# Hybrid mixer of a one-core, three-layer kernel: convolution taps from PSUM, and side work queued at other steps

## The chip, the cores and the metric

The kernel runs on one core of a Trainium2 chip as a single program. The metric is device time in microseconds (us) of that core. Before the change the median of three runs is 1608.9 us (1607.36 to 1610.53). Engines are named as the profile names them: PE is TensorE (PEld its weight loads), DVE is VectorE, ACT is ScalarE, POOL is GpSimd, SP is SyncE, which issues most DMAs.

## The reference, cut to what matters

Three layers follow each other on 256 tokens of width 1024, float32: a hybrid mixer (with 16 meta tokens ahead, so 272 positions), a PEER layer that gathers 256 rows of a 128 MB table per token, and a two-layer block of retention and stick-breaking attention. The change lies in the mixer alone:

```python
proj = hn @ w_in
q, k, v, g_out, g_low, z, xbc, dt_raw, gate_a, gate_b = split_cols(proj, IN_SPLITS)
o = gla_chunked(...)                                  # gated linear attention, 4 heads
o = rmsnorm(o, gla_norm_w) * jax.nn.silu(hd(g_out, GLA_DV))
y_a = o.reshape(Bsz, L, GLA_VW) @ w_up_gla
xbc = jax.nn.silu(causal_dwconv(xbc, conv_w, conv_b)) # 4 taps per channel
xs, Bm, Cm = split_cols(xbc, (SSD_D_INNER, SSD_BC, SSD_BC))
y = ssd_chunked(xs * dt, a, Bm, Cm) + d_skip * xs     # state space model, 4 groups of 8 heads
y = rmsnorm(y * jax.nn.silu(z))                       # per group
y_b = y @ w_up_ssd
mixed = jax.nn.sigmoid(gate_a) * y_a + jax.nn.sigmoid(gate_b) * y_b
h = h + mixed @ w_out
```

`causal_dwconv` forms, for each of 3072 channels, the sum over four taps of the input shifted by 3, 2, 1 and 0 positions times a weight, plus a bias.

## The kernel before, in words

The kernel streams its weights through the core as chunks of 128x1024 float32. SP loads a chunk, ACT copies it to a rounded half (`whi`, L221), DVE forms the remainder (`wlo`, L222), and PE multiplies each of its eight 128x128 blocks three times (`triple`, L260: high by high, high by low, low by high). The split of a chunk is issued four chunks ahead of its use. A chunk of kind T (`stream_T`) puts 24 matmuls of 272 or 256 columns into a PSUM bank, one of a ring of four (banks 0 to 3); a chunk of kind N (`stream_N`) makes 12 matmuls of 512 columns into two banks. When a bank is complete, a function (`use`) issues the work that empties it and returns the point from which the bank is free again.

The rest of the mixer (everything that isn't a product with streamed weights) is written as Python generators, the **sides**. Each `yield` ends a step; `side_step` runs the next step of the first side in the list, after a chunk, and, if `ring["steps"]` is 2, also in its middle. All engines take their instructions in the order in which this program issues them, so the number of `yield`s between two pieces of side work says how many half chunks of streamed work PE has between them. `until(key)` runs steps at once until that piece of work has been issued.

The order of the chunks in the mixer: 17 T chunks (small projections, k, q, v), 8 N chunks (g_out), 8 T chunks for B and C of the state space model, 32 T chunks in which the 16 gates and the 16 channel tiles of `xs` alternate (`GATES_XS`: 6 gates, then 10 times xs and gate, then 6 xs), 8 T chunks (`w_up_gla`), 16 N chunks (z), 16 T chunks (`w_up_ssd`, the second up-projection) and 8 N chunks (`w_out`).

The sides that the change touches, in their order:

- `gla_side`: the chunked linear attention. L588 to L598 form scaled q and k on DVE (`prod` is the last, L598); `attention(i)` multiplies them on PE (40 rows of 128x64, L319), ACT and DVE mask the scores (L633 to L636), PE multiplies them by v; then norms (L654, `rstd`, L660) and `features`, which turns the result on PE (`tr`, L322) and splits it into XH and XL.
- `conv` (a `use`): for a finished bank of B, C or xs, ACT copies the bank to the buffer XP behind three zeros (L716), ACT writes the last tap and the bias (L718), and three DVE instructions add the taps that look back, read from XP (L720). The bank is free after L718. A silu (L710) follows at the next chunk's `use`.
- `first_side` and `decays(g)`: 16 Abs (L757), one Exp (L762) and two products (L765) that build the decay masks M of a group.
- `ssd_side(g)`, for g = 0 to 3, queued when the fourth xs tile of group g is done: three `turn`s of x on PE (L322), the DVE products with dt (L797, L800, L802), L815 for the state, the state and output matmuls, and L826 to L843 on DVE. It also steps `decays(g + 1)`.
- `use_z`: silu of z (L895), product (L899), squares (L900), then `y_side(g)`: `rstd`, two diagonal matrices (L334, L335), and `turned`, eight matmuls whose results are split into the inputs of `w_up_ssd`.

## Time and profile before

| what | value |
|---|---|
| median of the runs shown | 1608.9 us |
| the profiled execution's own time | 1608.27 us |
| its span, first to last instruction | 1606.5 us |
| PE busy / DVE busy / ACT busy, share of the span | 86% / 67% / 46% |
| mean granted TensorE clock | 0.958 of full |

The span has three parts. The mixer and the projections run from 0 to about 487 us; from there to about 1130 us the PEER layer gathers table rows (DMA engines full, some 420 GB/s); the second block follows. In the rows, `idle before <-releaser` in square brackets is the time that an engine stood still before an instruction and the instruction that ended this wait.

### The profile page before, as it was taken

Reading aid. Unit: us, or ns where it says so; the run is one execution under the profiler, and the core shown is the slowest. Engines: PE = TensorE matmul, PEld = TensorE weight load, DVE = VectorE, ACT = ScalarE, POOL = GpSimd, SP = SyncE. Lnnn points to the kernel's source line nnn. Section 1 sums busy time; section 2 is a strip of 40 time slices with the busy share of each in tenths; the row PEclk is TensorE's granted clock in tenths of the full one; section 3 lists DMA queues with packets and bytes.
Section 4 is the critical chain, followed back from the end, with each engine's and each line's share of the span. In section 5 each row is a group of like instructions: output and inputs, shape, how many; then the busy total and the mean of one; then the engine's idle time right before and its main releaser. Section 6 shows DMA issues by size and latency. Waiting matters only on the chain. (4 is left out here: it accounts for less than half of the span.)

```text
span 1606.5 us, 18967 instructions
## 1 busy us (share of the span) xinstructions
PE 1379.1 (86%) x6549; PEld 993.4 (62%) x6549; DVE 1080.7 (67%) x2061; ACT 736.5 (46%) x1276; POOL 301.8 (19%) x260
## 2 busy tenths in 40 slices
PE   6998979999998787777777877778899999899987
PEld 5987978888988433233333333323497787888766
DVE  5767467875678787677777777665695465645554
ACT  5665777747454322222222222212454475567853
POOL 0000000000003564444444444443100000000000
PEclk9998999999999899989999999999999999899989
DMA  6452444444558999999999999999664456354442
GB/s 225 122 183 84 153 132 142 138 141 156 182 200 326 411 421 421 422 422 420 422 421 421 422 421 422 422 420 422 251 202 155 133 184 206 124 155 146 144 128 79
DMA packets 77806, 417.70 MB, mean 260 GB/s; under 512 B 8768, under 2 KB 8832, under 8 KB 44688
## 3 DMA queue, kind: packets, MB, share of 16 engines
q0 software_dynamic: 36864, 268.45, 40.3%
q1 hardware_dynamic: 40848, 148.06, 28.9%
q8 instruction: 52, 0.85, 0.2%
q14 instruction: 42, 0.34, 0.1%
HBM read 415.39 MB, written 1.08 MB: 259 GB/s over the span
## 5 line engine op out<-in xcount | busy, mean ns | idle before, releaser
L319 PE MATMUL ps<-AR 128*128 128x512 f32 (+6 forms) x1160 | 363.6, 465 | 106.5 <-ACT AR L1211 71.8
L222 DVE TENSOR_TENSOR wlo<-raw,whi 128x1024 fp32r<-128x1024 f32 x257 | 311.7, 1222 | 170.5 <-ACT whi L221 167.9
L319 PEld LDWEIGHTS ps<-AR 128*128 128x128 f32 (+2 forms) x1160 | 191.1, 198 | 269.5 <-issue 127.1
L221 ACT ACTIVATE whi<-raw 128x1024 fp32r<-128x1024 f32 x257 | 269.4, 1054 | 119.4 <-PE ps L260 99.3
L260 PE MATMUL ps<-XH,whi 128*128 128x256 f32 (+1 forms) x1032 | 306.6, 297 | 4.7 <-DVE XL L330 2.4
L319 PE MATMUL ps<-SLAB,AR 128*128 128x512 f32 x516 | 247.3, 633 | 66.7 <-ACT AR L1211 66.6
L260 PE MATMUL ps<-XL,whi 128*128 128x256 f32 (+1 forms) x1032 | 297.2, 288 | 0.0
L260 PE MATMUL ps<-XH,wlo 128*128 128x256 f32 (+1 forms) x1032 | 297.1, 288 | 0.0
L1176 POOL DMA_INDIRECT AR<-in_peer_uv,C x127 | 148.2, 1167 | 658.0 <-DVE C L1130 486.3
L319 PEld LDWEIGHTS ps<-SLAB,AR 128*128 128x128 f32 x516 | 101.2, 200 | 209.3 <-issue 120.3
L260 PEld LDWEIGHTS ps<-XH,whi 128*128 128x128 f32 x1032 | 201.1, 195 | 12.8 <-DVE XL L330 5.1
L260 PEld LDWEIGHTS ps<-XL,whi 128*128 128x128 f32 x1032 | 200.7, 194 | 0.9 <-issue 0.7
L1185 DVE CUSTOM_DVE_ANT_0 SLAB<-SLAB,AR 128x1024 f32<-128x1024 f32 x129 | 156.7, 1222 | 65.9 <-DMA SLAB<-in_peer_uv,C 65.9
L260 PEld LDWEIGHTS ps<-XH,wlo 128*128 128x128 f32 x1032 | 200.3, 194 | 0.0
L260 PE MATMUL ps<-whi,XH 128*128 128x512 f32 x480 | 197.4, 411 | 0.0
L1185 DVE CUSTOM_DVE_ANT_0 AR<-AR 128x1024 f32<-128x1024 f32 x127 | 154.3, 1222 | 55.4 <-DMA AR<-in_peer_uv,C 55.4
L260 PE MATMUL ps<-wlo,XH 128*128 128x512 f32 x480 | 188.7, 393 | 0.0
L260 PE MATMUL ps<-whi,XL 128*128 128x512 f32 x480 | 188.5, 393 | 0.0
L1176 POOL DMA_INDIRECT SLAB<-in_peer_uv,C x129 | 153.4, 1189 | 173.6 <-PE ps L319 131.8
L1211 ACT ACTIVATE AR<-C 128x128 f32<-128x128 f32 x254 | 84.0, 392 | 170.7 <-DVE C L1199 149.1
L1194 ACT ACTIVATE C<-C,SM 128x4 f32<-128x4 f32 (+2 forms) x72 | 21.4, 297 | 295.3 <-DVE C L1185 295.2
L260 PEld LDWEIGHTS ps<-whi,XL 128*128 128x128 f32 x480 | 90.8, 189 | 20.3
(243 smaller groups left out, 1187.8 us busy)
## 6 DMA issues: line engine op xcount, KB each, us to landing
raw<-in_stream SPq DMA_DIRECT2D x257, 512.0 KB, 4.2
AR<-scr SPq DMA_DIRECT2D x8, 512.0 KB, 5.2
SLAB<-in_peer_uv,C POOLq DMA_INDIRECT x129, 28.4
AR<-in_rows SPq DMA_DIRECT2D x4, 512.0 KB
AR<-in_peer_uv,C POOLq DMA_INDIRECT x127, 28.0
AR<-in_con SPq DMA_DIRECT2D x1, 1280.0 KB, 7.2
AR<-in_xin SPq DMA_DIRECT2D x2, 512.0 KB, 5.2
AR<-in_xin SPq DMA_DIRECT2D x1, 1024.0 KB, 8.7
```

Source lines behind the costliest of these rows:

```text
L221: a = A(lambda e: e.activation(h[:, :], r, ACT.Copy), loaded[i], free, chain=False)
L222: b = V(lambda e: e.tensor_tensor(l[:, :], r, h[:, :].bitcast(F32), ALU.subtract), a, loaded[i], free, chain=False)
L260: tok = PE(lambda e, s=s, m=m, n=n: e.matmul(out_ap, s, m, start=first and n == 0, stop=last and n == 2), *(after if n == 0 else ()), sign ...
L319: return PE(lambda e: e.matmul(out_ap, l, r, start=start, stop=stop, skip_group_check=onto), *after, signal=sig)
L1176: G(lambda e: e.indirect_dma_start(slots[j], None, peer_uv, bass.IndirectOffsetOnAxis(ap=col, axis=0)).then_inc(s, 16), idx_pt[m // 16], f ...
L1185: dot_pt[m] = V(lambda e: e.tensor_tensor_reduce(u, u, HN[:, i, :], 1.0, 0.0, ALU.mult, ALU.add, AV[:, i, at:at + 1]), uv_in[m], chain=False)
L1194: gelu_pt[ms[0]] = A(lambda e: e.activation(CC[:, i, c], AV[:, i, c], ACT.Gelu_apprx_tanh, scale=SM[:, 24 + i:25 + i]), dot_pt[ms[-1]])
L1211: a = A(lambda e: e.activation(d, ident, ACT.Copy, scale=CC[:, i, c]), c_ready, dg_free.get(m - 4), chain=False)
```

## The change

The change has four parts.

1. `conv` no longer copies the bank. The XP buffer, its zeros and L716 go; the three taps read the PSUM bank `o` itself, with outputs shifted by 3, 2 and 1 positions, and the bank is free after the last of them.
2. `stream_T` can run a third step in a chunk, after its sixth block, where `ring["steps"]` is 3. It is set to 3 when the first group of the state space model is queued, and back to 2 ahead of the second up-projection. In N chunks there are still two steps.
3. `yield`s are added: two after `prod`, one ahead of each `features` in `gla_side`, three at the start of each `ssd_side` and six inside it, two in `y_side` for the first three groups.
4. `until("yT7")` is called at the end of z, so the second `y_side` is issued there at the latest, and ahead of the last group's norm.

```diff
--- before.py
+++ after.py
@@ -287,6 +287,8 @@
                                 while mid:
                                     mid.pop(0)()
                                 side_step(2)
+                            if k == 5:
+                                side_step(3)
                         used[i] = tok
                         if kg == kt - 1:
                             bank_free[b] = use(o, tok)
@@ -598,8 +600,8 @@
             prod = V(lambda e: e.tensor_tensor(chunked(qS[:, :, :], 1), qE1[:, :, :, :],
                                                chunked(GX[:, :, X], 0)[:, :, :, 63:64].broadcast_to([128, 4, 2, 64]), ALU.mult))
             att_zero = V(lambda e: e.memset(attS[64:128, :, :, 0:64], 0.0))
-            yield
-            yield
+            for _ in range(4):
+                yield
 
             def features(i, v):
                 for g in range(2):
@@ -640,6 +642,7 @@
                 yield
                 if i == 1:
                     yield
+                    yield
                     yield from held
                 for h in range(4):
                     o = ps[5 + h // 2][:, (h % 2) * 256:(h % 2) * 256 + 256]
@@ -664,6 +667,7 @@
                     held = features(i, v)
             yield
             yield
+            yield
             yield from features(1, v)
 
 
@@ -683,7 +687,6 @@
 
         BT = place("BT", 22224, 4 * T).rearrange("p (g t) -> p g t", g=4)
         CT = place("CT", 23312, 4 * T).rearrange("p (g t) -> p g t", g=4)
-        XP = place("XP", 24400, 552).rearrange("p (b t) -> p b t", b=2)
         XSG = place("XSG", 24952, 2176).rearrange("p (b f t) -> p b f t", b=2, f=4)
         GA = place("GA", 7120, 2048).rearrange("p (f t) -> p f t", f=8)
         GB = place("GB", 9168, 2048).rearrange("p (f t) -> p f t", f=8)
@@ -697,9 +700,7 @@
         IN = place("IN", 20432, 512)
         ZS = place("ZS", 20944, 1024).rearrange("p (b c) -> p b c", b=2)
 
-        xp_free = [None, None]
         cbm_zero = None
-        v0 = V(lambda e: e.memset(XP[:, :, 0:3], 0.0), x_ready)
 
         late = []
 
@@ -712,16 +713,15 @@
         def conv(f, dst, first_free):
 
             def use(o, tok):
-                p = f % 2
-                a = A(lambda e: e.copy(XP[:, p, 3:3 + T], o), tok, xp_free[p], v0)
                 w = P_CONVW + 4 * f
-                a = d = A(lambda e: e.activation(dst, o, ACT.Identity, bias=par_(P_CONVB + f), scale=par_(w + 3)), first_free())
+                d = A(lambda e: e.activation(dst, o, ACT.Identity, bias=par_(P_CONVB + f), scale=par_(w + 3)), tok, first_free())
                 for j in range(3):
-                    v = V(lambda e, j=j: e.scalar_tensor_tensor(dst, XP[:, p, j:j + T], par_(w + j), dst, ALU.mult, ALU.add), d)
-                xp_free[p] = v
+                    late_by = 3 - j
+                    v = V(lambda e, j=j, n=late_by: e.scalar_tensor_tensor(dst[:, n:T], o[:, 0:T - n], par_(w + j), dst[:, n:T],
+                                                                           ALU.mult, ALU.add), d)
                 silu()
                 late.append((f, dst, v))
-                return a
+                return v
             return use
 
         def cons_gate(dst, key):
@@ -781,8 +781,8 @@
         def ssd_side(g):
             x = XSG[:, g % 2, :, :]
             Mg = M[:, g % 2, :, :, :]
-            yield
-            yield
+            for _ in range(5):
+                yield
             silu()
             cs = [pts[f"c{4 * g + j}"] for j in range(4)]
 
@@ -810,12 +810,16 @@
             yield
             pts[f"xsg{g}"] = turn(1, 7, 144)
             yield
+            yield
+            yield
             tok = mm(ps[6][:, :], BN[0:16, 2, 128 * g:128 * g + 128], XE[0:16, 1, :], True, True, True, xe[2], bank_free[6], pts["bn"])
             s_ready = bank_free[6] = A(lambda e: e.copy(SS[:, :], ps[6][:, :]), tok, pts.get("pe_ssd"))
             xe[0] = V(lambda e: e.tensor_tensor(heads(XE[:, 0, :]), heads(XD[:, 0, :]), each(STN[:, 0, 32 + 8 * g:40 + 8 * g]), ALU.mult))
             next(ahead, None)
             yield
+            yield
             next(ahead, None)
+            yield
             yield
             for i in range(2):
                 cols = slice(16 + 128 * i, 144 + 128 * i)
@@ -832,6 +836,7 @@
                     STN[:, i, 64 + 8 * g:72 + 8 * g].unsqueeze(2).broadcast_to([128, 8, 64]), ALU.mult), tok)
                 next(ahead, None)
                 yield
+                yield
                 next(ahead, None)
                 yield
                 for r in range(8):
@@ -869,6 +874,7 @@
                     until(f"xsg{f // 4 - 2}")
                 r = inner(o, tok)
                 if f % 4 == 3:
+                    ring["steps"] = 3
                     sides.append(ssd_side(f // 4))
                 return r
             return use
@@ -916,7 +922,7 @@
             yield
             while g > 1 and "z_done" not in pts:
                 yield
-            for _ in range(4 if g == 3 else 2):
+            for _ in range(4):
                 yield
             for j in range(4):
                 f = 4 * g + j
@@ -930,6 +936,7 @@
 
         stream_N(4, 8, 0, T, NM, x_ready, use_z)
         pts["z_done"] = PE.now()
+        until("yT7")
         last = y_side(3)
         next(last)
         sides.append(last)
@@ -966,6 +973,7 @@
                 yield
 
         sides.append(mix_side())
+        ring["steps"] = 2
         stream_T([(0, TX, cons_yb(f)) for f in range(8)], y_at, TX, yt_ready)
         side_all()
         mix_features()
```

The program's order shows what moved. First DVE, around the first `attention`, from the split two chunks ahead of it. L598 is `prod`, L720 the taps, L635 and L636 mask the scores. Before:

```order
L222 TENSOR_TENSOR wlo_58<-raw,whi_53 128x1024
L598 TENSOR_TENSOR AR<-AR 128x8x64
L600 MEMSET AR 64x8x64
L720 SCALAR_TENSOR_TENSOR AR<-AR,PAR 128x272 x3
L222 TENSOR_TENSOR wlo_54<-raw,whi_49 128x1024
L635 COPY_PREDICATED AR<-C,ps 64x4x64
L636 COPY_PREDICATED AR<-C,ps 64x4x64
```

And now (`prod` is L600, the masks L637 and L638):

```order
L222 TENSOR_TENSOR wlo_58<-raw,whi_53 128x1024
L600 TENSOR_TENSOR AR<-AR 128x8x64
L602 MEMSET AR 64x8x64
L720 SCALAR_TENSOR_TENSOR AR<-ps,PAR,AR 128x269
L720 SCALAR_TENSOR_TENSOR AR<-ps,PAR,AR 128x270
L720 SCALAR_TENSOR_TENSOR AR<-ps,PAR,AR 128x271
L222 TENSOR_TENSOR wlo_54<-raw,whi_49 128x1024
L720 SCALAR_TENSOR_TENSOR AR<-ps,PAR,AR 128x269
L720 SCALAR_TENSOR_TENSOR AR<-ps,PAR,AR 128x270
L720 SCALAR_TENSOR_TENSOR AR<-ps,PAR,AR 128x271
L222 TENSOR_TENSOR wlo_55<-raw,whi_50 128x1024
L637 COPY_PREDICATED AR<-C,ps 64x4x64
```

The masks have moved back by one chunk: two groups of taps and two splits now stand between `prod` and them, where there was one of each.

Second ACT, from the end of the first group's Abs (L757) to the silu of the fourth xs tile, for which the first `turn` of group 0 waits (the last row of each). Before, behind the last Abs:

```order
L221 ACTIVATE whi_52<-raw 128x1024
L762 ACT_TABLE_LOAD
L762 ACTIVATE AR<-AR 128x2048
L729 ACTIVATE AR<-ps 128x256
L710 ACT_TABLE_LOAD
L710 ACTIVATE AR<-AR 128x272
L221 ACTIVATE whi_53<-raw 128x1024
L716 COPY AR<-ps 128x272
L718 ACTIVATE AR<-ps,PAR 128x272
L221 ACTIVATE whi_49<-raw 128x1024
L729 ACTIVATE AR<-ps 128x256
L710 ACTIVATE AR<-AR 128x272
```

And now:

```order
L757 ACTIVATE AR<-AR 128x128 x4
L717 ACTIVATE AR<-ps,PAR 128x272
L757 ACTIVATE AR<-AR 128x128 x4
L221 ACTIVATE whi_49<-raw 128x1024
L762 ACT_TABLE_LOAD
L762 ACTIVATE AR<-AR 128x2048
L729 ACTIVATE AR<-ps 128x256
L711 ACT_TABLE_LOAD
L711 ACTIVATE AR<-AR 128x272
```

The mask work has moved back by two chunks, so that the silu of that tile now comes straight behind the Exp, where two chunks of other work stood between them.

Third ACT, at the end of z: L895 and L900 are `use_z` of the last group, L329 splits a turned feature, L349 is a square root of `rstd`. Before:

```order
L895 ACT_TABLE_LOAD
L895 ACTIVATE AR<-ps 128x512
L900 ACTIVATE AR,SM<-AR 128x512
L895 ACTIVATE AR<-ps 128x512
L900 ACTIVATE AR,SM<-AR 128x512
L349 ACT_TABLE_LOAD
L349 ACTIVATE SM<-SM 128x2
L221 ACTIVATE whi_52<-raw 128x1024
```

And now:

```order
L901 ACT_TABLE_LOAD
L901 ACTIVATE AR<-ps 128x512
L906 ACTIVATE AR,SM<-AR 128x512
L901 ACTIVATE AR<-ps 128x512
L906 ACTIVATE AR,SM<-AR 128x512
L331 ACTIVATE XH<-ps,PAR 128x256 x4
L351 ACT_TABLE_LOAD
L351 ACTIVATE SM<-SM 128x2
```

The four splits of group 1 (features 4 to 7 of the second up-projection's input) now stand behind the last `use_z`; before, they had been issued six N chunks earlier.

## Rows read from the trace of the kernel before

**Rows 1.** Busy time by stretch: PE, PEld, DVE, ACT, POOL, granted clock, DMA share, GB/s.

```profile
85.00:424.00 339.00, 307.06 (x2125) 279.79 (x2125) 231.80 (x353) 223.78 (x361) 0.00 (x0) 0.96 0.44 141
```

**Rows 2.** Timeline of POOL: start, duration, instruction, idle before it and releaser.

```profile
486.74 2.00 POOL L1176 DMA_INDIRECT AR<-in_peer_uv,C  x1 [486.29 <-DVE C L1130]
```

**Rows 3.** Timeline of PE: side work that PE stood waiting for, 85 to 424.

```profile
132.74 2.82 PE L319 MATMUL ps<-AR 128*64 128x64 f32 x40 [4.25 <-DVE AR L598]
...
156.43 0.66 PE L322 MATMUL ps<-C,AR 128*128 128x128 f32 x4 [2.58 <-DVE AR L660]
...
173.10 0.66 PE L322 MATMUL ps<-C,AR 128*128 128x128 f32 x4 [2.09 <-DVE AR L660]
...
212.77 1.12 PE L322 MATMUL ps<-C,AR 128*128 128x128 f32 x4 [9.03 <-ACT AR L710]
...
250.59 1.08 PE L322 MATMUL ps<-C,AR 128*128 128x128 f32 x4 [3.68 <-ACT AR L710]
...
285.97 0.63 PE L322 MATMUL ps<-C,AR 128*128 128x128 f32 x4 [1.01 <-ACT AR L710]
...
293.21 1.12 PE L319 MATMUL ps<-AR 16*128 16x512 f32 x2 [1.22 <-DVE AR L797]
...
301.47 1.57 PE L319 MATMUL ps<-AR 128*128 128x512 f32 x6 [1.72 <-DVE AR L815]
...
354.10 1.16 PE L319 MATMUL ps<-AR 128*128 128x128 f32 x8 [1.13 <-DVE AR L335]
...
368.79 1.59 PE L319 MATMUL ps<-AR 128*128 128x128 f32 x8 [2.89 <-DVE AR L335]
```

**Rows 4.** Timeline of PE: three streamed matmuls after the restart at 250.59.

```profile
253.06 0.40 PE L260 MATMUL ps<-XL,whi 128*128 128x272 f32 x1
253.29 0.30 PE L260 MATMUL ps<-XH,wlo 128*128 128x272 f32 x1
253.42 0.29 PE L260 MATMUL ps<-XH,whi 128*128 128x272 f32 x1
```

**Rows 5.** Groups of DVE from 85 to 460: busy us, mean ns, idle before them.

```profile
L222 DVE TENSOR_TENSOR wlo<-raw,whi 128x1024 fp32r<-128x1024 f32 x92 | 111.7, 1221 | 48.8 <-ACT whi L221 48.6
L720 DVE SCALAR_TENSOR_TENSOR AR<-AR,PAR 128x272 f32<-128x272 f32 x72 | 36.1, 502 | 20.0 <-ACT AR L718 17.3
...
L660 DVE SCALAR_TENSOR_TENSOR AR<-ps,SM,AR 128x256 f32<-128x256 f32 x8 | 3.9, 484 | 0.3
```

**Rows 6.** Groups of ACT from 85 to 460, same columns as rows 5.

```profile
L221 ACT ACTIVATE whi<-raw 128x1024 fp32r<-128x1024 f32 x92 | 96.0, 1050 | 39.6 <-PE ps L260 38.2 <-DMA raw<-in_stream 1.3
L757 ACT ACTIVATE AR<-AR 128x128 f32<-128x128 f32 x64 | 25.8, 402 | 3.0 <-DMA AR<-scr 1.0
L718 ACT ACTIVATE AR<-ps,PAR 128x272 f32<-128x272 f32 x24 | 13.9, 578 | 0.8
...
L716 ACT COPY AR<-ps 128x272 f32<-128x272 f32 x24 | 9.3, 387 | 22.8 <-PE ps L260 21.9
...
L762 ACT ACT_TABLE_LOAD x4 | 5.1, 1283 | 0.1
```

**Rows 7.** Timeline of DVE around the first attention.

```profile
119.87 1.23 DVE L222 TENSOR_TENSOR wlo<-raw,whi 128x1024 fp32r<-128x1024 f32 x1 [0.57 <-ACT whi L221]
...
132.00 0.69 DVE L598 TENSOR_TENSOR AR<-AR 128x512 f32<-128x512 f32 x1
...
136.62 0.44 DVE L635 COPY_PREDICATED AR<-C,ps 64x256 f32<-64x256 uint32 x1 [0.46 <-ACT AR L634]
```

**Rows 8.** Timeline of ACT from the first group's Abs to the silu.

```profile
189.23 1.06 ACT L221 ACTIVATE whi<-raw 128x1024 fp32r<-128x1024 f32 x1
...
212.28 0.43 ACT L710 ACTIVATE AR<-AR 128x272 f32<-128x272 f32 x1 [1.73 <-DVE AR L720]
```

**Rows 9.** Timeline of ACT at the end of z: last use_z, first and last.

```profile
388.94 1.28 ACT L895 ACT_TABLE_LOAD   x1
...
394.46 0.18 ACT L900 ACTIVATION_READ_ACCUMULATOR AR<-AR 128x1 f32 x1
```

## The prediction

> **What bounds the kernel now.** I read the busy time by stretch first, because the change touches one stretch only. From 85 to 424 us, from the projections to the second up-projection, PE is busy for 307.06 of 339 us, DVE for 231.80 and ACT for 223.78 [rows 1]. PE is the bound there, and the most that a better order can win is PE's idle time, 31.9 us, and what the clock costs. Does a microsecond won there arrive at the end? The first gather of the PEER layer starts at 486.74, after POOL has waited 486.29 us for an index that DVE computes from the mixer's result [rows 2]. Nothing of that layer starts before the mixer is done, so I take a gain in the mixer as a gain at the end, one for one.
>
> Next I read PE's timeline for the side work that it stood waiting for. Ten waits stand in it [rows 3], 29.6 us of the 31.9. The reader should see two things: each wait is of PE at a piece of side work, never at a streamed chunk, and the releaser is ACT or DVE, which were behind by less than the wait, while PE had more chunks to multiply. In groups: the attention and its features 4.25 + 2.58 + 2.09 = 8.9; the first turn of group 0, 9.03; of group 1, 3.68; group 2, 1.01 + 1.22 + 1.72 = 3.95; the two first turns of `y_side` 1.13 + 2.89 = 4.0.
>
> A wait also slows what follows it. After the restart at 250.59 the streamed matmuls start 0.23 us apart and then, from 253.29 on, 0.13 apart [rows 4]: the half-speed level (1.2 GHz) and the full one (2.4 GHz). The mean granted clock of the stretch is 0.96 [rows 1], so of 339 us some 0.08 x 339 = 27 were at half speed, and the loss is at most half of that, 13.6 us; part of it fell into the idle time. I take 10 us for it, by the same share as the waits that go.
>
> A chunk of 24 matmuls of 272 columns takes 24 x 0.13 = 3.1 us at full clock [rows 4], one of 256 columns 256/272 of that, 2.9. An N chunk, 12 matmuls of 512 columns, has as many columns as the latter and is taken as long.
>
> **The copies.** The 24 copies to XP took 387 ns each, 9.3 us of ACT [rows 6]. ACT is not the bound, so their going is worth something only where PE waits for ACT. The 72 taps stay on DVE. What does one cost with its operand in PSUM? The nearest row is L660, the same operation with PSUM input and a pointer scalar, 484 ns for 256 columns; L720 from SBUF takes 502 ns for 272 [rows 5]. Sixteen columns more, at the 1.19 ns that a column of L222 takes at most, make 484 into 503. I take no change; the bounds are 10 ns less and 100 ns more per tap. The Trainium skill speaks against this part: VectorE: DVE Perf Modes, section Rules for kernel authors, has one copy PSUM to SBUF first where many operations follow, and Perfetto Trace Analysis, section Optimizing Scalar/DVE Operations, gives DVE an access overhead of about 60 ns on SBUF and 125 ns on PSUM; by that, an estimate of mine, 72 x 65 ns = 4.7 us of DVE would come on top. The rows of this case show no such difference. The bank is now free after the third tap, on DVE, and no longer after ACT's second instruction: about 1.6 us and a place in DVE's queue later. PE comes back to a bank three chunks later, about 9 us; that covers it as long as DVE's taps end within 9 us of their chunk.
>
> **The attention.** It now comes one chunk later. DVE is the late one: it had one gap of 0.57 us ahead of 119.87 and then worked without one until `prod` ended at 132.69 [rows 7]. It does the same work in the same order now, so PE's wait falls from 4.25 to about 4.25 - 3.1 = 1.2. But then a wait comes that was not there. The masks stand behind two groups of taps and two splits now, where it was one of each: 3 x 0.53 + 1.25 = 2.85 us more. Before, the masks began at 136.62 after 0.46 of idle [rows 7] and took 0.9, two of 0.44. Now they begin at about 136.2 + 2.85 = 139.0 and end at 139.9, while PE, after 2.8 us of scores [rows 3], half of that at full clock, and half a chunk (1.5), is there at 135.6 to 137.1. That is 2.8 to 4.3 us; I take 3.5. The first `features` gain half a chunk (1.5 us) and the end of the taps' competition, and wait 0.4 in place of 2.58 (bounds 0 and 1.1); the second gain half a chunk, 0.6 in place of 2.09. In sum 8.9 becomes 5.7, **-3.2**.
>
> **Group 0.** The mask work and the first turn both move back by two chunks, so the length of PE's path between them stays 5.5 chunks. ACT's path gets shorter. From the split ahead of the Abs at 189.23 to the end of the silu at 212.71 it was 23.5 us [rows 8]. In the new order two splits (2 x 1.05), one pair of conv instructions and one more copy (0.97 + 0.39), one gate and one silu (0.4 each) have left this piece [rows 6, 8], and the silu no longer waits 1.73 for taps that stood behind the mask products: 6.0 us less, so 3.0 of the 9.03 stay. Where DVE's wait remains it is 4.7, where ACT is a little less behind 2. I take 2.5, **-6.5**.
>
> **Group 1.** Its turn comes 2.25 chunks later, 6.6 us against a wait of 3.68. What is late next: Exp and two table loads (1.28 each) [rows 6] now stand right ahead of the silu, but the turn has 2.75 chunks, 8 us, after that silu's place. I take no wait, **-3.7** (bound: 1 us stays).
>
> **Group 2.** Its turn comes 2.5 chunks later, after the last xs tiles, so 1.01 and 1.22 go. But group 1's work now lies in the stretch in which each chunk brings taps. DVE has 3 x 0.53 + 1.25 = 2.85 per chunk and group 1's products, and is behind: the wait of the state matmul for L815 (1.72) stays in another place, some 1.9, and a second one of 0.6 at group 2's. 3.95 becomes 2.5, **-1.5** (bounds: 0 and 5 remain).
>
> **The turns of `y_side`.** Two steps more are an N chunk, 2.9 us, as long as the longer wait, 2.89; both waits go, -4.0. The second side now falls to the end of z. Its four splits stand behind the last `use_z` on ACT, which took from 388.94 to 394.64, 5.7 us [rows 9]. That starts about 1.4 before PE ends z (half a chunk) and now some 0.7 late; a split takes about 0.5 on each of ACT and DVE, by L718 and L660 [rows 5, 6]. So feature 4 is there -1.4 + 0.7 + 5.7 + 1.0 = 6.0 us after the end of z. PE has the eight matmuls of the turn (1.6, the last of rows 3) and half a chunk (1.4) to do: it waits 3.0, and 0.6 for features 5 to 7. Half a microsecond more goes to the third side, which now ends just as its features are wanted. **+0.1**, by itself no gain (bounds: -3 and +3).
>
> **Sum.** -3.2 - 6.5 - 3.7 - 1.5 + 0.1 = -14.8 us of idle time. That is half of the 29.6, so half of the clock's 10 us goes too: -5. Together -20. The profiled execution took 1608.27 us (span 1606.5 and 1.8 around it), 0.6 below the median of the runs shown, 1608.9; I forecast against the median: 1608.9 - 20 = **1589 us**.
>
> **Rivals.**
>
> - Everything is hidden: the new waits after the attention and at z's end do not come, and the clock stays up. 29.6 to about 32 with the clock: 1578. For it: DVE and ACT are busy for two thirds of the stretch. Against: DVE's queue around the attention has no slack in the order.
> - The waits come back behind DVE: mask products after the attention at their bound (4.3, at half speed), group 0 at 4.7, group 2 at 5, z's end at +3. About 9 to 10 us are left of the gain: 1599.
> - A tap from PSUM costs 100 ns more. That is 7.2 us of DVE; on the path lie the 15 or so taps around the attention and as many before group 2's turn, 3 us, and banks come free later: 1592. Against it stands L660 [rows 5]. This is the rule of the Trainium skill, Perfetto Trace Analysis, section Optimizing Scalar/DVE Operations, with a larger price than the page's.
> - Slower: the banks. A conv bank comes free only behind DVE's queue. If DVE's taps end more than 9 us after their chunk, PE waits at the streamed chunk itself; at 10.5 us on average, 1.5 us for each of the 24 conv chunks, that is +36 against -20: 1625. It decides from 9 us on. Against: ACT ran 9 us behind before group 0's turn and PE waited at the turn, not at a bank.
> - The change does what it says by the program's order, so that it does nothing is left with a small chance: waits that only change places.
>
> **How the numbers follow.** Forecast (-14 to -26) 0.50; everything hidden 0.17; behind DVE 0.20; dearer taps 0.04; no difference 0.04; the banks 0.05. A difference of under 0.2% (3.2 us) can't be told from none by a measurement of this kernel. Faster 0.91, same 0.04, slower 0.05. The range takes in the forecast's bounds, most of the two neighbours and stops at -32 and -7: 1577 to 1602, some 0.83 of the chance.
>
> **What would show it.** In the profile after: no L716 group; the taps with PSUM input at 0.49 to 0.51 us; PE's idle ahead of the first turn of group 0 at 2 to 5 us and ahead of group 1's none; a new wait of PE for the masks (L638) of 3 to 4 us behind the first attention; a wait of 3 us for XL a few matmuls after the end of z; the first gather at about 467. It would be wrong if PE waited at streamed matmuls (L260) for taps, if a tap took 0.6 us, or if the gather came 20 us earlier and the end did not.

## The result, and the profile after

The changed kernel takes 1598.47 us (median of four runs, 1597.76 to 1600.19), the kernel before 1609.72 in the same series (1607.36 to 1611.12). The ratio is 0.994, 95% interval 0.9928 to 0.9952: 7.7 to 11.6 us of 1609.7 less. The time lies inside the stated range, but the gain is half of the 20 us that were forecast, and it came out where the rival "the waits come back behind DVE" stood (1599).

Two executions also differ in places that the change doesn't touch, so I measure the mixer by itself, from the first matmul of the decay gates (32x32, the last side work ahead of anything that moves) to the first gather. That **stretch** took 486.74 - 95.93 = 390.8 us before [rows 2] and 475.18 - 93.53 = 381.7 after: 9.2 us less. The start-up ahead of it was 2.4 us shorter in the second execution, where DVE had the first input rows 1.2 us sooner, and what follows the gather 1.0 longer.

The window of [rows 1] in the profile after (its start and end, length, busy us of PE, PEld, DVE, ACT and POOL with instructions, granted clock, DMA share, GB/s), cut where the second up-projection has come as far:

```profile
85.00:413.00 328.00, 305.89 (x2117) 277.56 (x2116) 229.50 (x346) 210.83 (x334) 0.00 (x0) 0.96 0.46 144
```

PE idles for 22.1 us, where it was 31.9. The granted clock is still 0.96: what the forecast had expected from the clock didn't come. The waits of PE in it (timeline of PE, the answer to [rows 3]), and the gather of [rows 2] on POOL:

```profile
129.46 1.61 PE L321 MATMUL ps<-AR 128*64 128x64 f32 x40 [0.77 <-DVE AR L600]
136.73 4.53 PE L321 MATMUL ps<-AR 128*128 128x256 f32 x12 [3.52 <-DVE AR L638]
...
171.82 0.66 PE L324 MATMUL ps<-C,AR 128*128 128x128 f32 x4 [2.41 <-DVE AR L663]
...
206.89 1.11 PE L324 MATMUL ps<-C,AR 128*128 128x128 f32 x4 [4.43 <-ACT AR L711]
...
232.83 2.00 PE L321 MATMUL ps<-AR 128*128 128x64 f32 x16 [0.79 <-DVE AR L848]
...
251.00 1.12 PE L321 MATMUL ps<-AR 16*128 16x512 f32 x2 [0.95 <-DVE AR L797]
258.70 1.57 PE L321 MATMUL ps<-AR 128*128 128x512 f32 x6 [0.24 <-DVE AR L817]
...
290.95 2.07 PE L321 MATMUL ps<-AR 16*128 16x512 f32 x2 [4.19 <-DVE AR L797]
...
378.11 0.39 PE L260 MATMUL ps<-XH,whi 128*128 128x256 f32 x1 [2.75 <-DVE XL L332]
```

```profile
475.18 2.00 POOL L1184 DMA_INDIRECT AR<-in_peer_uv,C  x1 [474.74 <-DVE C L1138]
```

The masks' wait, 3.52, is the one that the prediction put at 3.5, and z's end, 2.75, the one put at 3. The other two large ones are where it went wrong: group 0's turn at 4.43 in place of 2.5, and group 2's state matmul at 4.19, larger than the three waits of group 2 before (3.95). All waits together went from 29.6 to 20.2 us; 0.19 of this, at 371.88, isn't shown. The taps, by their groups of DVE (busy us, mean ns, idle before them), have one form for each shift:

```profile
L720 DVE SCALAR_TENSOR_TENSOR AR<-ps,PAR,AR 128x271 f32<-128x271 f32 x24 | 12.0, 500 | 0.8
L720 DVE SCALAR_TENSOR_TENSOR AR<-ps,PAR,AR 128x270 f32<-128x270 f32 x24 | 12.0, 498 | 0.8
L720 DVE SCALAR_TENSOR_TENSOR AR<-ps,PAR,AR 128x269 f32<-128x269 f32 x24 | 11.9, 497 | 9.0 <-ACT AR L717 7.3
```

From PSUM a tap takes 497 to 500 ns, from SBUF it took 502 [rows 5]: no price. (By the Trainium skill, Perfetto Trace Analysis, section Optimizing Scalar/DVE Operations, each would be about 65 ns dearer, an estimate from the two overheads given there; the measurement decides.)

Why is group 0 still late? ACT's timeline ahead of that turn (the answer to [rows 8]):

```profile
187.32 1.06 ACT L221 ACTIVATE whi<-raw 128x1024 fp32r<-128x1024 f32 x1
190.84 1.71 ACT L757 ACTIVATE AR<-AR 128x128 f32<-128x128 f32 x4 [2.45 <-DMA AR<-scr]
...
206.41 0.43 ACT L711 ACTIVATE AR<-AR 128x272 f32<-128x272 f32 x1
```

From the split to the end of the silu ACT needs 19.5 us, where the prediction had 23.5 - 6.0 = 17.5. What it didn't have is the wait of the first Abs for the broadcast load of the decays (tensor `scr`). In the kernel before such loads held ACT up for 1.0 us in the whole stretch [rows 6], 0.40 of it here. SP's timeline shows when this one was issued, before and then after:

```profile
184.85 0.90 SPq L201 DMA_DIRECT2D AR<-scr  x2
```

```profile
184.07 0.90 SPq L201 DMA_DIRECT2D AR<-scr  x2
```

ACT came to the Abs 5.4 us behind that issue before (at 190.29, the end of its split) and comes 4.3 us behind it now (at 188.38). The load landed 5.8 us behind its issue before (190.69) and 6.8 now (190.84). So of the 2.05 us by which the wait grew 1.1 are ACT's coming sooner behind the issue, and 0.9 the load's taking longer.

Group 1's load is late in the same way, and the 0.79 at 232.83, which is for group 0's last product, follows from it. ACT's timeline:

```profile
227.34 1.71 ACT L757 ACTIVATE AR<-AR 128x128 f32<-128x128 f32 x4 [2.14 <-DMA AR<-scr]
```

Behind these Abs stands a split, and behind DVE's half of it the sum L848 that PE wants. In seven kernels (the change and runs 2, 3, 7, 9, 11 and 12 below) ACT waits 1.60 to 2.21 us for this load, and PE's wait for that sum is each time 1.34 to 1.36 us less (2.14 and 0.79 here, 2.21 and 0.87 in run 12); where ACT waits 1.19 us or less (runs 4, 6 and 8) PE doesn't wait there. (In runs 5 and 10 the order is another there.) No run moved this load.

And group 2's state matmul? ACT and then DVE in the 6 us ahead of it:

```profile
286.94 0.43 ACT L711 ACTIVATE AR<-AR 128x272 f32<-128x272 f32 x1 [2.37 <-DVE AR L720]
287.27 2.93 ACT L221 ACTIVATE whi<-raw 128x1024 fp32r<-128x1024 f32 x3
```

```profile
285.34 1.56 DVE L720 SCALAR_TENSOR_TENSOR AR<-ps,PAR,AR 128x269 f32<-128x269 f32 x3
288.34 1.23 DVE L222 TENSOR_TENSOR wlo<-raw,whi 128x1024 fp32r<-128x1024 f32 x1 [1.44 <-ACT whi L221]
289.68 0.42 DVE L890 SCALAR_TENSOR_TENSOR AR<-AR,ps 128x256 f32<-128x256 f32 x1
290.20 0.69 DVE L797 TENSOR_TENSOR AR<-ps,SM 128x512 f32<-128x512 f32 x1
```

The two engines wait for each other in turn: ACT's silu for the taps of the last xs tile, three splits behind the silu, DVE for one of these splits, and only then comes the product L797 that PE wants. Which of these is the cause, and whether a wait that goes is a gain, the experiments had to say.

### The profile page after: what moved, and what is told of

Same layout as the page of the kernel before. It is cut to its first block and busy times, and to the rows that moved or that the text cites. A ratio compares the mean times of both kernels' runs of the same rounds, so it can differ in the third digit from the quotient of the medians.

```text
span 1595.9 us, 18934 instructions
## 1 busy us (share of the span) xinstructions
PE 1386.3 (87%) x6549; PEld 995.0 (62%) x6549; DVE 1080.1 (68%) x2060; ACT 725.0 (45%) x1250; POOL 304.0 (19%) x260
## 5 line engine op out<-in xcount | busy, mean ns | idle before, releaser
L321 PE MATMUL ps<-AR 128*128 128x512 f32 (+6 forms) x1160 | 376.5, 475 | 106.8 <-ACT AR L1219 73.0
L321 PEld LDWEIGHTS ps<-AR 128*128 128x128 f32 (+2 forms) x1160 | 194.6, 200 | 277.3 <-issue 133.1
L321 PE MATMUL ps<-SLAB,AR 128*128 128x512 f32 x516 | 243.1, 625 | 57.9 <-ACT AR L1219 57.9
L1184 POOL DMA_INDIRECT AR<-in_peer_uv,C x127 | 152.3, 1199 | 655.9 <-DVE C L1138 474.7
```

The source lines that it names most:

```text
L321: return PE(lambda e: e.matmul(out_ap, l, r, start=start, stop=stop, skip_group_check=onto), *after, signal=sig)
L1184: G(lambda e: e.indirect_dma_start(slots[j], None, peer_uv, bass.IndirectOffsetOnAxis(ap=col, axis=0)).then_inc(s, 16), idx_pt[m // 16], f ...
```

## The experiments

My theory when they began: what is left of the waits is ACT's and DVE's lag at two places, behind the late load and behind the late taps, and the clock follows the waits. The rivals: the copies are the gain; or the waits only move. Twelve kernels ran. "Ratio" is to the kernel before, on the same chip in the same series; the stretch is that of the profiled execution. Against the change, only the intervals of runs 1, 4, 11 and 12 lie clear of its own; what the other runs gain or lose against it is within the noise of the medians and is read from the traces. There, too, executions differ ahead of the place where an edit acts, by up to 1.7 us (run 8), so the stretch alone settles no smaller difference.

| kernel | median us | ratio, 95% interval | stretch us |
|---|---|---|---|
| the change | 1598.47 | 0.9940 (0.9928 to 0.9952) | 381.7 |
| 1 taps only | 1606.05 | 0.9987 (0.9977 to 0.9997) | 388.6 |
| 2 order only | 1600.17 | 0.9949 (0.9932 to 0.9966) | 385.1 |
| 3 loads earlier | 1595.90 | 0.9930 (0.9907 to 0.9953) | 379.4 |
| 4 no late taps | 1592.81 | 0.9908 (0.9892 to 0.9925) | 374.9 |
| 5 masks later | 1598.78 | 0.9931 (0.9910 to 0.9953) | 382.0 |
| 6 group 2 later | 1601.12 | 0.9949 (0.9933 to 0.9966) | 384.4 |
| 7 wait filled | 1596.18 | 0.9922 (0.9903 to 0.9941) | 379.6 |
| 8 last silu later | 1595.66 | 0.9923 (0.9907 to 0.9940) | 378.1 |
| 9 third step in z | 1595.34 | 0.9920 (0.9904 to 0.9937) | 379.4 |
| 10 masks later, with copies | 1599.80 | 0.9945 (0.9929 to 0.9962) | 385.3 |
| 11 edits of 3, 8, 9 | 1592.53 | 0.9897 (0.9880 to 0.9914) | 376.2 |
| 12 11 and filled | 1592.83 | 0.9903 (0.9888 to 0.9919) | 372.9 |

### Taps or order (1 and 2)

The first is the kernel before with part 1 of the change alone (the edit of `conv` in the diff above), the second the changed kernel without it.

> The kernel before with the conv change alone (taps from PSUM, no copy to XP; every step where it was). Theory: the copies were worth something only where PE waits for ACT. The first turn of group 0 waited 9.03 us for ACT's silu; three or four copies of 0.39 us and the table loads beside them leave the way to it, so 6 to 8 us of that wait stay; the waits for DVE (4.25, 2.58, 2.09, 3.68) stay as they are. Time 1 to 3 us under the kernel before, taps at 0.49 to 0.51 us, no wait of PE at streamed matmuls for a bank. Rival, the copies are the gain: 7 us or more under the kernel before, group 0's wait under 5. Rival, the banks: later release at the old order makes PE wait at L260 for DVE, and the time is not under that of before.

> The changed kernel with the copies to XP put back (taps from SBUF, bank free after ACT's second instruction); all the moved and added steps stay. Theory: the steps carry nearly all of the gain; ACT has 9.3 us more to do, and PE's wait at group 0's turn grows from 4.43 by the four to six copies in its way, 1.5 to 2.5 us, group 2's by about 1; the rest stays. Time 1599 to 1603, that is 2 to 4 us over the changed kernel. Rival, the copies are the gain: 1605 or more. Rival, the copies cost nothing because ACT has slack wherever PE waits: within 1 us of the changed kernel.

Taps alone give 0.13% (2.1 us; the stretch 2.2), the order alone 0.51% (8.2; 5.7), both 0.6%. So the order carries most of it, as the theory had it. PE's timeline, taps only and then order only:

```profile
208.25 1.12 PE L322 MATMUL ps<-C,AR 128*128 128x128 f32 x4 [7.90 <-ACT AR L707]
...
296.76 1.57 PE L319 MATMUL ps<-AR 128*128 128x512 f32 x6 [3.56 <-DVE AR L811]
```

```profile
208.16 1.11 PE L324 MATMUL ps<-C,AR 128*128 128x128 f32 x4 [4.63 <-ACT AR L714]
...
293.36 2.07 PE L321 MATMUL ps<-AR 16*128 16x512 f32 x2 [5.63 <-DVE AR L801]
```

Without copies group 0's wait is 7.90 for 9.03 [rows 3], but the state update behind group 2's turn waits 3.56 for 1.72. With copies in the new order group 0 waits hardly longer (4.63 for 4.43; I had expected 6 to 7), since ACT, later by its copies, waits less for the load (1.82 us there); the difference stands at group 2, 5.63 for 4.19.

### Group 0's load (3)

```diff
         def decays(g):
             Mg = M[:, g % 2, :, :, :]
-            load_bc(g)
+            if g:
+                load_bc(g)
...
             nonlocal cbm_zero
+            load_bc(0)
```

> The changed kernel with the two broadcast loads of group 0 issued at the start of first_side, three side steps earlier. Theory: ACT's 16 Abs of group 0 waited 2.45 us for these loads (0.40 in the kernel before), since ACT now comes there earlier than they land; this wait is on the path to the silu and the first turn of group 0. With the loads earlier it is under 0.5, PE's wait at L324 for L711 falls from 4.43 to about 2 to 2.5, and the time by 2 to 3 us. Rival: the silu waits for DVE's taps or for the table load behind Exp in any case, so that the turn still waits over 3.5 and the time stays within 0.7 us; or the loads land no earlier because they stand behind weight loads in SP's queue, and ACT still waits 2 us.

ACT, and then PE, in this kernel:

```profile
189.97 1.06 ACT L221 ACTIVATE whi<-raw 128x1024 fp32r<-128x1024 f32 x1
191.12 1.71 ACT L758 ACTIVATE AR<-AR 128x128 f32<-128x128 f32 x4
...
206.70 0.43 ACT L711 ACTIVATE AR<-AR 128x272 f32<-128x272 f32 x1
```

```profile
207.19 0.66 PE L324 MATMUL ps<-C,AR 128*128 128x128 f32 x4 [2.09 <-ACT AR L711]
```

The wait for the load is gone, split to silu takes 17.2 us (forecast 17.5), the turn waits 2.09 (forecast 2.5), and the clock is 1.00 from 200 to 225 us where it was 0.86. But this execution differs in another place too: from 145 to 200 us its clock was 0.97 and not 1.00, so PE itself came to the turn 1.5 us later after the stretch's start, and a part of the shorter wait is that. Run 12 has the same edit at 1.00: PE comes to the turn 108.9 us into the stretch, as in the changed kernel, and the turn starts at 111.0 where it was 113.4. There too split to silu takes 17.2 us. So the late load is worth 2.35 us at the turn. (The clock from 200 to 225 us is 0.93 there.) As a time, 0.9930 against 0.9940 is too close to tell apart.

### Group 2's state matmul (4, 6 and 8)

Run 4 leaves out the DVE taps of the last four xs tiles, so its result isn't the function any more:

```diff
                     late_by = 3 - j
+                    if f in (12, 13, 14, 15):
+                        v = d
+                        continue
```

> The changed kernel without the 12 DVE taps of the last four xs tiles (channels 1536 to 2047 of the convolution keep only their last tap); all else is issued. Theory: at group 2's state matmul PE waits 4.19 us because DVE is behind by the taps of features 12 to 15, and ACT, whose silus and splits stand between them, with it. Without these 6 us of DVE work the wait is under 1.5, and the time 2.5 to 4.5 us less. Rival: ACT's Exp of the masks and the table loads around it (some 5 us at 273 to 278) hold both queues up: the wait stays at 3 or more and the time falls by less than 1.5.

```profile
286.47 1.12 PE L321 MATMUL ps<-AR 16*128 16x512 f32 x2 [0.28 <-DVE AR L800]
```

The wait falls to 0.28, the clock from 285 to 305 is 1.00 for 0.83, and the ratio falls from 0.9940 to 0.9908 (5.1 us). Exp and its table loads stayed where they were, so they are not what holds PE up there. The late taps are.

Run 6 gives that matmul four steps more:

```diff
             yield
+            if g == 2:
+                for _ in range(4):
+                    yield
             tok = mm(ps[6][:, :], BN[0:16, 2, 128 * g:128 * g + 128], XE[0:16, 1, :], True, True, True, xe[2], bank_free[6], pts["bn"])
```

> The changed kernel with four more steps (a chunk and a third, 4.1 us) between group 2's turns and its state matmul alone. Theory: the wait of 4.19 us there is only DVE's and ACT's lag behind the late taps, and goes with the clock's fall behind it (full clock from 285 to 305 us in place of 0.83); what comes later, group 3 and y_side, has that much slack except at z's end, where the forced second side waits 2.75 and may wait 1 to 2 us more. Time 3 to 5 us under the changed kernel. Rival: the waits move whole, z's end at 6 or more or the z chunks wait for group 3's result, and the time stays within 1 us.

```profile
290.42 1.12 PE L321 MATMUL ps<-AR 16*128 16x512 f32 x2 [0.71 <-DVE AR L797]
...
311.89 2.00 PE L321 MATMUL ps<-AR 128*128 128x64 f32 x16 [2.05 <-DVE AR L851]
377.19 3.78 PE L321 MATMUL ps<-AR 128*128 128x128 f32 x16 [7.55 <-DVE AR L337]
```

The rival was right. The wait goes, and at the last streamed matmul of z PE is 3.4 us ahead of the changed kernel (368.34 - 93.97 = 274.4 us into the stretch, for 277.8). But 7.55 us at z's end come in place of 2.75: the second `y_side` is now so late that the call at z's end has to issue its diagonals there, and PE waits for both of them.

Run 8 takes away a link of the ping-pong and no steps. The last silu goes behind the next chunk's split:

```diff
         stream_T([(xs if which else gates).pop(0) for which in GATES_XS], 0, T, x_ready)
-        silu()
         until("ox")
...
                 pts[f"mx{f}"] = V(lambda e: e.scalar_tensor_tensor(GA[:, f, :], GA[:, f, :], 1.0, o, ALU.add, ALU.mult), tok, pts[f"ga{f}"])
+                silu()
```

> The changed kernel with the last silu of the convolution (tile 15) issued one chunk later, at the first use of the up-projection's chunks, behind that chunk's split and no longer ahead of three splits. Theory: ACT stands 2.37 us for the taps of tile 15 ahead of three splits, DVE then waits 1.44 for a split and comes to the product L797 late; with the silu out of the way PE's wait at group 2's state matmul falls from 4.19 to 2 to 2.7, and the time by 1.5 to 3 us. Rival: DVE's own queue (taps, splits, products) is the longer chain, so that the wait stays over 3.5 and the time within 0.7 us.

```profile
288.41 1.12 PE L321 MATMUL ps<-AR 16*128 16x512 f32 x2 [2.78 <-DVE AR L797]
```

The wait went as expected, 2.78 for 4.19; by the ratio, 0.9923, the time falls by some 2.7 us. The stretch is 3.6 us shorter, but not all of this is the edit's: 0.8 had come by group 0's turn, where the load held ACT up for 1.62 us and not 2.45, and 1.7 by the start of the first up-projection, which still lies ahead of the silu.

### The masks and the banks (5 and 10)

```diff
                 v = bank_free[7] = attention(i)
                 yield
+                if i == 0:
+                    yield
+                    yield
```

> The changed kernel with two more steps (one chunk, 3.1 us) between the first attention's scores and the products of the masked scores with v; all later side steps of the mixer's first half move back by the same. Theory: PE waited 3.52 us for DVE's second mask (L638), because it had half a chunk of its own between scores and product; with a whole chunk more 0.4 to 1 of it is left, and the features and group 0's turn wait no longer than now. Time 2 to 3.5 us under the changed kernel. Rival: the chunk put in between brings taps and a split of its own ahead of the masks (2.85 us of DVE), so that the wait stays at 3 or more; or the wait moves to the features (2.41 becomes 5) and the time stays within 0.7 us.

PE, and DVE ahead of the third of PE's waits:

```profile
137.90 3.29 PE L321 MATMUL ps<-AR 128*128 128x256 f32 x14 [0.73 <-DVE AR L638]
...
200.97 0.66 PE L324 MATMUL ps<-C,AR 128*128 128x128 f32 x4 [0.25 <-ACT AR L714]
...
211.03 0.57 PE L260 MATMUL ps<-XH,whi 128*128 128x272 f32 x1 [5.73 <-DVE AR L723]
...
367.69 0.39 PE L260 MATMUL ps<-whi,XL 128*128 128x512 f32 x1
375.60 3.78 PE L321 MATMUL ps<-AR 128*128 128x128 f32 x16 [7.52 <-DVE AR L337]
```

```profile
205.12 1.23 DVE L222 TENSOR_TENSOR wlo<-raw,whi 128x1024 fp32r<-128x1024 f32 x1 [7.43 <-ACT whi L221]
206.38 2.48 DVE L768 TENSOR_TENSOR AR<-AR 128x1024 f32<-128x1024 f32 x2
209.32 1.57 DVE L723 SCALAR_TENSOR_TENSOR AR<-ps,PAR,AR 128x269 f32<-128x269 f32 x3 [0.46 <-DVE AR L768]
```

The last streamed matmul of z in the changed kernel, for the fourth line:

```profile
371.31 0.39 PE L260 MATMUL ps<-whi,XL 128*128 128x512 f32 x1
```

The masks' wait went, 3.52 to 0.73, and group 0's with it, 4.43 to 0.25. Part of it came back at once: PE, now earlier, stood 5.73 us at a **streamed** matmul, for a tap. DVE had waited 7.43 us for a split behind ACT's Abs and Exp, did two mask products, and only then the taps; PE needed the bank of these taps. In the changed kernel PE reaches this place late enough not to see it. So group 0 is limited by ACT and DVE, and an earlier arrival of PE there keeps only a part of its worth: of the 2.8 us won at the masks 1.8 are left by the chunk ahead of group 1's turn. Group 2 waits less too (2.42 for 4.19), and at the last streamed matmul of z PE is 4.8 us ahead of the changed kernel (367.69 - 94.68 = 273.0 us into the stretch, for 371.31 - 93.53 = 277.8). All of that is lost at z's end, where it waits 7.52 us, as in run 6. Neither run was tried with more steps in z (run 9), so what their gains are worth without that wait stays open.

Run 10 is this kernel with the copies to XP (a bank then comes free on ACT, ahead of the taps).

> The kernel of the masks two steps later, with the copies to XP put back, so that a convolution bank is free after ACT's second instruction and not after DVE's third tap. In the version without copies PE waited 5.73 us at a streamed matmul (L260) for a tap, at 211 us, behind Exp on ACT. Theory: that is the bank of a convolution tile, held until DVE has done the taps; with the copies the bank is free some 4 to 5 us sooner, and this wait is 1.5 or less, though ACT has more to do; part of it comes back at the state matmul behind it (L801). Rival: PE stands there for a split or for the turn in any case, and the wait stays at 4 or more, for another releaser.

```profile
208.02 0.39 PE L260 MATMUL ps<-XH,whi 128*128 128x272 f32 x1 [1.07 <-DVE wlo L222]
217.37 2.07 PE L321 MATMUL ps<-AR 16*128 16x512 f32 x2 [6.80 <-DVE AR L804]
```

The wait for the bank is gone; what is left, 1.07, is for a split. That settles that it was the bank. But the state matmul behind it waits 6.80 for 1.15: the lag of DVE is paid in either form, and the ratio is no better (0.9945, with the same 7.52 us at z's end).

### The clock (7), and z's end (9)

```diff
+            if g == 2:
+                for n in range(16):
+                    mm(ps[6][:, :], XH[:, 0:128], XH[:, 128:640], True, True, False, bank_free[6])
             tok = mm(ps[6][:, :], BN[0:16, 2, 128 * g:128 * g + 128], XE[0:16, 1, :], True, True, True, xe[2], bank_free[6], pts["bn"])
```

> The changed kernel with 16 matmuls of 512 columns that nobody reads, ahead of group 2's state matmul, in the time in which PE waits there. Some 16 x 0.23 = 3.7 us of work in a wait of 4.19. Theory: it is the wait that lets the clock fall (0.83 granted from 285 to 305 us, half speed from 293 to 297); with PE busy the granted clock stays at 1.00 there, the wait that is left is under 0.8, the state matmul starts at the same time to within 0.3 us, and the time falls by 1.5 to 2.5 us for the clock alone. Rival: the clock falls in any case or the fall costs nothing because DVE and ACT, which are late, set the pace behind it: time within 0.7 us of the changed kernel.

The window from 285 to 305 us, of the changed kernel and then of this one (columns as above):

```profile
285.00:305.00 20.00, 15.81 (x93) 13.14 (x92) 16.52 (x24) 8.50 (x14) 0.00 (x0) 0.83 0.57 187
```

```profile
285.00:305.00 20.00, 18.83 (x125) 15.78 (x124) 17.22 (x25) 7.66 (x12) 0.00 (x0) 1.00 0.55 185
```

```profile
292.31 1.12 PE L321 MATMUL ps<-AR 16*128 16x512 f32 x2 [0.37 <-DVE AR L797]
```

The state matmul starts 197.5 us into the stretch, as without the filler (197.4): work that nobody reads has won nothing there. But the clock stays at 1.00, and by z's end PE is 1.7 us ahead, at the gather 2.1. That is the price of this wait beside its own length. The ratio, 0.9922, fits it, but its interval overlaps that of the change.

Run 9 gives z's chunks a third step:

```diff
-                        if tt == 0:
-                            side_step(2)
+                        side_step(2 if tt == 0 else 3)
```

> The changed kernel with the third side step in z's chunks too (an N chunk made two steps, now three). Theory: all sides stand in one list, and what is put between two pieces moves every later piece; the second y_side reaches z's end because the list has too few steps there, and the wait of 2.75 us for XL with the half speed behind it comes from that. With eight or more steps gained in z the second y_side is done ahead of z's end: the wait of 2.75 goes, and the time falls by 2.5 to 4 us. Rival: the group's products then come sooner than DVE and ACT can follow, and PE waits 2 us or more in z for L848, L817 or L337: time within 0.7 us or longer.

```profile
352.35 1.16 PE L320 MATMUL ps<-AR 128*128 128x128 f32 x8 [1.01 <-DVE AR L336]
...
393.82 0.38 PE L260 MATMUL ps<-XH,whi 128*128 128x256 f32 x1 [1.37 <-DVE XL L331]
```

The 2.75 and the half speed behind it are gone; 1.01 comes at the first `y_side`, and 0.6 more at 393.82. The ratio is 0.9920, some 3 us less: the list was short of steps in z.

### Together (11 and 12)

> The changed kernel with three of the edits together: group 0's loads earlier, the last silu one chunk later, the third step in z's chunks. Theory: they act at three places (group 0's turn, group 2's state matmul, z's end) and add up: 5 to 9 us under the changed kernel, 1590 to 1594. Rival: the waits move from one to the next, as with the masks two steps later and with group 2 four steps later, and the sum is less than the best of them alone, under 3 us.

0.9897 (0.9880 to 0.9914), an interval that lies wholly under that of the change: this version beats both kernels, by 16.6 us and by about 7. By the medians the three edits add up: alone they gave 1.6, 2.7 and 3.2 us. By the stretch they don't wholly: 2.3, 3.6 and 2.3 us alone, 5.5 together.

> The three edits together, and 11 matmuls of 512 columns that nobody reads ahead of group 2's state matmul, 11 x 0.23 = 2.5 us in a wait of 2.79. Theory: the clock stays at 1.00 from 285 to 305 us where it was 0.83 granted in the version without them, the wait left is under 0.6, and the time falls by 1 to 2.5 us to 1590 to 1591.5. Rival: with the wait of 2.79 already short, what the clock gives back goes into the next wait (the state update L818 or the second norm L336), and the time stays within 0.7 us of the version without them.

```profile
205.06 0.66 PE L323 MATMUL ps<-C,AR 128*128 128x128 f32 x4 [2.09 <-ACT AR L710]
```

```profile
285.00:305.00 20.00, 19.20 (x130) 15.97 (x128) 16.18 (x22) 10.62 (x20) 0.00 (x0) 1.00 0.59 203
```

The wait at the state matmul is gone, the clock is at 1.00, and the gather comes 3.3 us earlier in the stretch than in run 11. The medians don't show it (1592.83 and 1592.53). In the profiled execution the part behind the last gather took 477.7 us, 2.9 more than in run 11. Whether that is chance stays open.

## Why the prediction was right or wrong

**Copies and taps: right.** A tap was put at 502 ns and took 497 to 500, and the copies alone were worth 2.1 us. That this comes only where PE waits for ACT isn't shown: in run 1 the wait for `prod`, for DVE, fell too, from 4.25 to 3.80.

**The attention, -3.2, measured -2.2.** The wait for `prod` (1.2, measured 0.77), the new one for the masks (3.5, measured 3.52) and the first features (0.4, none) were right. The second features were put at 0.6 and waited 2.41, in every kernel of the new order that ran. By the trace the norm's squares on ACT (L657, from 164.04 on) stand behind a gate (L729) that has waited 4.62 us for PE's own chunk, so the added step seems to have moved the chain and its user alike. That was not tried by itself.

**Group 0, -6.5, measured -4.6 at its turn and +0.8 behind it: the first failed step is ACT's path,** 6.0 us shorter by the list of instructions. The list was right (17.2 us in run 3), but it had no term for the wait for the load, 0.40 us before, and an engine that is less behind waits longer for it: 2.45 us. The rows showed a beginning of it [rows 6], 1.0 us of wait for this DMA, and the prediction didn't ask what would be late next there. The 0.79 behind the turn comes from group 1's load, 2.14 us late for ACT.

**Group 1, -3.7, measured -2.5.** The turn's wait went as forecast; 0.95 and 0.24 came behind it, for DVE, a little over the bound of 1 us.

**Group 2, -1.5, measured +0.2: the second failed step.** The text put DVE behind by "some 1.9, and 0.6"; it was 4.19, because the late taps, a silu and three splits chain the two engines (runs 4 and 8). Counting DVE's work per chunk gave its load, not the order in which two queues wait for each other.

**`y_side`, +0.1, measured -1.1.** Its wait at z's end was put at 3.0 and was 2.75; the 0.6 and 0.5 beside it were nearly none.

**The clock, -5, measured about none: the third failed step.** "Half of the waits, so half of the clock's loss" was wrong. The waits fell by 9.4 us and the stretch by 9.2, so nothing is left that the clock gave. One minus the granted clock, times length, over ten windows from 85 to 424 us, sums to 14.0 us before and 12.1 after. The loss didn't follow the sum of the waits: the three groups kept their slow stretches (0.86 from 200 to 225 in both; 0.91 from 245 to 265 in both; 0.91 became 0.83 from 285 to 305), though group 0 and 1 waited less.

Together: of the forecast 20 us, 14.8 were waits and 5 the clock; the waits gave 9.4 and the clock nothing.

Of the rivals, "behind DVE" gave the time, though group 0 was late for a load and not for DVE, and z's end, which it put at +3, gained 1.1: that its 1599 was met is in part luck. The bank rival, 0.05, didn't come with this change; its mechanism is real (runs 5 and 10) and shows as soon as PE comes to group 0 about 3 us earlier. What would show it: the missing L716, the taps and the three waits were as written; group 1's turn had none, but the gather came at 475 and not at 467. One reading was wrong, without consequence: PE did wait at streamed matmuls before, 0.76 us at 406.87 and 0.64 at 409.64, for XL; both are still there (0.74 and 0.64).

## What to carry to other kernels

When a wait is to be removed by handing the waiting engine more work, ask at each place who stands behind it: in one serial list of side work a step that is added early pushes the last item past its deadline, and an engine that is less behind meets the next late thing (a load, a bank). Forecast a late product along the chain through all the queues it passes, not by the load of one engine. And try edits that take a link out of such a chain (a load earlier, one silu later) before edits that add distance: they took nothing from later pieces, where distance (runs 5 and 6) won time and lost it again at z's end, where the list ran out of steps.

## What the runs showed of the hardware

The clock was the surprise. A wait of 0.95 us with a matmul of 16 rows behind it (251.00 in the profile after) was followed by half speed from 252.78 on: the next streamed matmuls start at 253.00 and 253.23, 0.23 us apart as in [rows 4]. A wait of 2.41 us ahead of the second features left the clock at 1.00 from 145 to 200 us in the changed kernel and in runs 2, 4, 5, 6, 8 and 12, and was followed by half speed (0.97 in that window) in runs 3, 7, 9, 10 and 11, though runs 3, 4, 6, 7, 8, 9, 11 and 12 have the same order of PE's work up to there. So which waits cost clock can't be read from their length alone, and one execution can't settle a difference of 1 to 2 us. The cost of one slow stretch was 1.7 to 2.1 us (run 7).

Another cost nothing. Behind the wait at 251.00 PE runs at half speed and comes to its next product at 258.70, 7.70 us later. Run 8 kept the full clock there (1.00 from 245 to 265 us, for 0.91), and the same two products are 7.70 us apart as well:

```profile
249.40 1.12 PE L321 MATMUL ps<-AR 16*128 16x512 f32 x2 [0.45 <-DVE AR L797]
257.10 1.57 PE L321 MATMUL ps<-AR 128*128 128x512 f32 x6 [1.74 <-DVE AR L817]
```

At full clock PE stands 1.74 us waiting for L817, at half speed 0.24: DVE sets the pace there, and what the clock takes comes off the wait.
